# The conditioning product beside the RWKV-7 prompt scan: column-tiled fp32 matmuls against a high/low split on GpSimd

## The reference, cut to what matters

```
mod = jax.nn.silu(c) @ lp['w_ada'] + lp['b_ada']          # (9, 1024) @ (1024, 6144)
fm = jax.nn.silu(c) @ w_ada_f + b_ada_f                   # (9, 1024) @ (1024, 2048)
```

```
def step(S, inp):
    r_t, d_t, k_t, v_t, kk_t, b_t = inp
    sk = jnp.einsum('bhvk,bhk->bhv', S, kk_t)
    S = S * d_t[:, :, None, :] - sk[..., None] * b_t[:, :, None, :] + v_t[..., None] * k_t[:, :, None, :]
    return S, jnp.einsum('bhvk,bhk->bhv', S, r_t)
```

## Time and profile before

| what | value |
|---|---|
| time, median of 3 | 4452.27 us |
| the profiled execution | 4452.27 us, span 4450.7 us |
| mean granted TensorE clock, whole span | 0.969 of full speed |
| phase of the change | 752 to 1085 us, 333 us |
| PE busy in the phase | 303.76 us |
| DVE, ACT, POOL busy in the phase | 153.09, 64.83, 1.38 us |
| product records on PE (L1354) | 256 |
| granted clock in the phase | 0.97 |

### The profile page before, as it was taken

The page is one execution under the profiler, slowest core; times in us unless marked ns, Lnnn a source line. Parts: engine busy times, 40 slices in busy tenths (PEclk is TensorE's granted clock), DMA queues, the critical chain, the costliest instruction groups (busy, mean ns, idle before and its releaser), DMA issues. The chain is left out here.

```text
span 4450.7 us, 85485 instructions
## 1 busy us (share of the span) xinstructions
PE 4178.9 (94%) x32575; PEld 3796.1 (85%) x32575; DVE 3177.0 (71%) x6008; ACT 1431.2 (32%) x2183; POOL 1364.5 (31%) x1063
## 2 busy tenths in 40 slices
PE   7999999988778989999999998899999999999997
PEld 4889888887547879878888887899999999999996
DVE  5631344444844248899976665899999999999997
ACT  2221222211644222233346674222222222222223
POOL 6433331000032200054433233333434434434430
PEclk9999999999869999999999999999999999999998
DMA  4655666555533311144435546899999999999994
GB/s 169 208 191 188 205 227 207 192 219 165 154 118 115 123 63 34 51 142 142 143 119 189 193 176 254 294 301 300 301 301 301 302 299 299 303 299 300 303 299 151
DMA packets 523004, 928.00 MB, mean 209 GB/s; under 512 B 284032, under 2 KB 351232, under 8 KB 518688
## 3 DMA queue, kind: packets, MB, share of 16 engines
q1 hardware_dynamic: 387024, 549.29, 37.5%
q0 software_dynamic: 80960, 346.96, 22.8%
q10 hardware_dynamic: 54816, 28.85, 2.2%
HBM read 785.79 MB, written 206.30 MB: 223 GB/s over the span
## 5 line engine op out<-in xcount | busy, mean ns | idle before, releaser
L3296 POOL DMA_INDIRECT ex_rows<-expert_rows,ex_here x512 | 585.5, 1144 | 962.9 <-DVE acc_tok L3431 871.8
L3431 DVE SCALAR_TENSOR_TENSOR acc_tok<-ex_rows,ex_wsp,acc_tok 128x1024 f32<-128x1024 f32 x512 | 634.0, 1279 | 0.2 <-issue 0.2
L2663 PE MATMUL ex_psa<-x_dense_high,eg_u_high 128*128 128x288 f32 x2048 | 605.4, 296 | 9.3 <-ACT ex_w L3359 6.2
L2663 PE MATMUL ex_psa<-x_dense_low,eg_u_high 128*128 128x288 f32 x2048 | 605.4, 296 | 0.0
L2663 PE MATMUL ex_psa<-x_dense_high,eg_u_low 128*128 128x288 f32 x2048 | 605.0, 295 | 0.0
L2754 POOL TENSOR_TENSOR eg_u_low<-eg_u,eg_u_high 128x1024 fp32r<-128x1024 f32 x130 | 330.3, 2541 | 800.0 <-ACT eg_u_high L2749 800.0
L3328 PE MATMUL ex_pso<-ex_w_high,ex_v_high 128*128 128x288 f32 x2048 | 440.9, 297 | 20.0 <-DVE acc L3413 19.6
L3359 ACT ACTIVATE ex_w<-ex_psa 128x288 f32<-128x288 f32 x256 | 105.2, 411 | 1056.0 <-PE ex_psa L2663 1046.8
L3328 PE MATMUL ex_pso<-ex_w_high,ex_v_low 128*128 128x288 f32 x2048 | 439.4, 296 | 0.0
L3328 PE MATMUL ex_pso<-ex_w_low,ex_v_high 128*128 128x288 f32 x2048 | 438.3, 296 | 0.0
L3413 DVE TENSOR_TENSOR acc<-ex_pso,acc 128x576 f32<-128x576 f32 x512 | 373.9, 751 | 47.7 <-PE ex_pso L3328 47.7
(11 more groups left out here) (510 smaller groups left out, 9214.7 us busy)
## 6 DMA issues: line engine op xcount, KB each, us to landing
eg_u<-in_u SPq DMA_DIRECT2D x256, 512.0 KB, 3.3
expert_rows<-in_v SPq DMA_DIRECT2D x128, 512.0 KB, 7.0
ex_v<-in_v SPq DMA_DIRECT2D x128, 512.0 KB
weights<-wt_stage SPq DMA_DIRECT2D x9, 4096.0 KB, 13.0
ex_g<-weights SPq DMA_DIRECT2D x128, 288.0 KB
expert_rows<-eg_act SPq DMA_DIRECT2D x256, 128.0 KB, 1.7
proj<-in_out POOLq DMA_DIRECT2D x50, 548.5 KB, 6.2
in_w<-in_w_in SPq DMA_DIRECT2D x50, 512.0 KB, 4.7
```

The costliest lines, as they stand in the source:

```text
L2663: yield nc.tensor.matmul(out[:, 0:b - a], w[:, kc, :], half[:, kc, a:b], start=n == 0, stop=n == len(passes) - 1)
L3296: pool.indirect_dma_start(rows[i][:, :], None, table, index(here[par][:, t, j:j + 1]), element_offset=ROW_RUNS[t][0]).then_inc(s_row[i], 16)
L3431: v.scalar_tensor_tensor(out=acc_tok[:, t, :], in0=rows[i][:, at:at + D], scalar=wsp[:, i:i + 1], in1=acc_tok[:, t, :], op0=ALU.mult, op1= ...
```

## The change

The product is now computed from fp32r operands, without column groups. `cond` becomes 18 columns wide: 9 with the high part of the silu'd vectors and 9 with the low part. The weights are split too: POOL makes `wah` (rounded copy, fp32r) and then `wal` (weights minus `wah`), which lies on the same bytes as `wa`. That is eight copies and eight subtractions of 128x384 for each of 16 chunks. PE multiplies the 18 columns by both, 16 matmuls of 384 columns a chunk into 18 partitions; `fold` is now 18x9 and adds the two halves. PE waits for the subtractions (`s_al`) where it waited for the load (`s_wa`), and each half of the product is now 8 matmuls of fp32r instead of 4 of fp32. `k.clear_retired()` moves behind the split of chunk 1 in POOL's queue.

```diff
-        wa = [sb(f"ada{i}", [P, KC, ADA_STEP * P]) for i in range(2)]
-        cond = sb("cond", [P, KC, COL_TILE])
-        fold = sb("fold", [P, COL_TILE])
+        wa, wal = zip(*[(sb(f"ada{i}", [P, KC, ADA_STEP * P]), k.twin(f"rwc_ada_low{i}", [P, KC, ADA_STEP * P])) for i in range(2)])
+        wah = [ctx.enter_context(nc.sbuf_tensor(f"rwc_ada_high{i}", [P, KC, ADA_STEP * P], F32R)) for i in range(2)]
+        cond = ctx.enter_context(nc.sbuf_tensor("rwc_cond", [P, KC, 2 * NCOND], F32R))
+        fold = sb("fold", [2 * NCOND, NCOND])
...
-        row = sb("ada_row", [P, ACOLS])
-        rowp = b.ps[:, BANK_MOD, 0:ACOLS]
+        row = sb("ada_row", [2 * NCOND, ACOLS])
+        rowp = b.ps[0:2 * NCOND, BANK_MOD, 0:ACOLS]
...
-                g.memset(cond[:, :, :], 0.0).then_inc(s_cond, 1)
-                pool.wait_ge(s_cond, 1)
                 g.tensor_copy(cond[:, :, 0:NCOND], k.cT[:, :, :]).then_inc(s_cond, 1)
-                for q in range(COL_TILES):
...
-                pool.wait_ge(s_cond, 2 + COL_TILES)
-                k.clear_retired()
+                g.tensor_tensor(fold[:, :], k.ident[0:2 * NCOND, 0:NCOND], k.ident[0:2 * NCOND, NCOND:2 * NCOND], ALU.add).then_inc(s_cond, 1)
+                pool.wait_ge(s_cond, 2)
+                g.tensor_tensor(cond[:, :, NCOND:2 * NCOND], k.cT[:, :, :], cond[:, :, 0:NCOND].bitcast(F32), ALU.subtract).then_inc(s_cond, 1)
+                for c in range(NCH):
+                    pool.wait_ge(s_wa[c % 2], 16 * (c // 2) + 16)
+                    for kc in range(KC):
+                        g.tensor_copy(wah[c % 2][:, kc, :], wa[c % 2][:, kc, :]).then_inc(s_ah, 1)
+                    for kc in range(KC):
+                        pool.wait_ge(s_ah, KC * c + kc + 1)
+                        g.tensor_tensor(wal[c % 2][:, kc, :], wa[c % 2][:, kc, :], wah[c % 2][:, kc, :].bitcast(F32),
+                                        ALU.subtract).then_inc(s_al, 1)
+                    if c == 1:
+                        k.clear_retired()
...
-                        rest = (nc.tensor.matmul(rowp[COL_TILE * q:COL_TILE * q + COL_TILE, :], cond[:, j + q, :], wa[h][:, j + q, :],
-                                                 start=j == 0, stop=j == KC - COL_TILES)
-                                for j in range(0, KC, COL_TILES) for q in range(COL_TILES))
+                        rest = (nc.tensor.matmul(rowp, cond[:, kc, :], part[:, kc, :], start=kc == 0 and part is wah[h],
+                                                 stop=kc == KC - 1 and part is wal[h])
+                                for kc in range(KC) for part in (wah[h], wal[h]))
...
-                        pe.wait_ge(s_wa[h], 16 * r + 16)
-                        pe.wait_ge(s_cond, 2 + COL_TILES)
+                        pe.wait_ge(s_al, KC * (2 * r + h + 1))
+                        pe.wait_ge(s_cond, 3)
...
-                        for _ in range(COL_TILES):
+                        for _ in range(KC):
                             next(rest)
...
-                            mm = nc.tensor.matmul(modp[:, m, :], row[:, m * P:(m + 1) * P], fold[:, 0:NCOND],
+                            mm = nc.tensor.matmul(modp[:, m, :], row[:, m * P:(m + 1) * P], fold[:, :],
                                                   start=True, stop=True)
```

More of the change, by code:

```diff
@@ L152, in lasting @@
         return self.ctx.enter_context(self.nc.sbuf_tensor(name, shape, dt))
-COL_TILE = 32
-COL_TILES = P // COL_TILE
 ADA_FIRST = 16
@@ L1262, in phase_rw_prompt @@
         s_init = k.sem("rwc_state_zeroed")
-        s_cond = k.sem("rwc_cond_padded")
+        s_cond = k.sem("rwc_cond_split")
+        s_ah = k.sem("rwc_ada_high_made")
+        s_al = k.sem("rwc_ada_low_made")
         heads = [(p_, rows) for p_ in range(NPAIR) for rows in halves()]
@@ L1337, in _ @@
                 g = nc.gpsimd
-                g.memset(cond[:, :, :], 0.0).then_inc(s_cond, 1)
-                pool.wait_ge(s_cond, 1)
                 g.tensor_copy(cond[:, :, 0:NCOND], k.cT[:, :, :]).then_inc(s_cond, 1)
-                for q in range(COL_TILES):
-                    part = slice(COL_TILE * q, COL_TILE * q + COL_TILE)
-                    pool.wait_ge(s_cond, 2 + q)
-                    g.tensor_copy(fold[part, :], k.ident[part, part]).then_inc(s_cond, 1)
-                pool.wait_ge(s_cond, 2 + COL_TILES)
-                k.clear_retired()
+                g.tensor_tensor(fold[:, :], k.ident[0:2 * NCOND, 0:NCOND], k.ident[0:2 * NCOND, NCOND:2 * NCOND], ALU.add).then_inc(s_cond, 1)
[11 more added lines that the diff above has]
+                        k.clear_retired()
             @block.tensor
```

## The result

The changed kernel takes 4471.68 us (median of 9 runs, 4467.71 to 4487.97) against 4452.27 us for the kernel before (9 runs on the same chip, 4439.77 to 4462.12). The ratio is 1.0055, with a 95% interval of 1.004 to 1.0069: 18 to 31 us more, 24.5 us by the ratio and 19.4 us by the two medians. The two differ because the ratio rests on more executions: the record has 38 of the changed kernel, 4460.05 to 4493.20 us with a median of 4476.9. It is slower, and less so than the forecast of 4486 us; it lies inside the range. The profiled execution after took 4473.9 us, its mean granted clock was 0.967.

A forecast was written before the change was run, and what follows sets the result against it. The prediction took PE to bound the phase and added 22.4 us for the longer product and 12 us for POOL beside DVE to 4452.3 us, giving 4487; it named 4486 us, own range 4474 to 4501, 8-in-10 range 4466 to 4504.

The forecast's parts named there:

- PE is the full queue: In the changed phase PE, busy 303.76 of 333 us, sets the pace; longer matmul groups are paid almost whole.
- The product, +22.4 us: Conditioning product on PE: each half takes 1.49 us, 0.70 more, over 32 halves; bounds +18.5 to +24.3 us.
- Fold, row copy and bias at nothing: Steps after the product: fold matmuls and ACT's copy out of PSUM cost nothing more; bias only moves with the product.
- POOL's split and the wait on it: POOL's copies and subtractions take 13.3 us a chunk; PE's wait for them never binds, 5 us of cover left.
- POOL beside DVE, +12 us: POOL's instructions block DVE lines with two SBUF inputs, delaying PE 1.7 us in each of seven rounds; bounds 3.5 to 24.
- The 0.5 for the `tmp` line of h = 1 itself: In each round, the DVE line the product waits for loses 0.5 us to a POOL instruction.
- The 0.2 a round for lines behind the product: Delay of DVE's `xy` and `ml` lines after the product, counted at 0.2 us a round.
- No other phase changed: Expected sign in the changed profile: this phase 30 to 38 us longer, all other phases as before.
- Hidden: Rival: PE's idle time and PE work absorb most of the extra time; 4452 to 4470 us, chance 0.18.
- DVE the bound: Rival: blocking hits every two-input DVE instruction on the chain, or PSUM readers too; about 4515 us, chance 0.10.
- The split late: Rival: POOL, held up by DVE, needs over 17.6 us a chunk and PE waits; about 4509 us, chance 0.05.
- Faster: Rival: longer matmuls remove PE's idle time from instruction supply, with the product's extra inside it; about 4430 us, chance 0.03.

The follow-up runs named there:

- e7: The changed kernel with every half product computed twice, the second pass overwriting the first with the same values; 4526.97 us, ratio 1.0179.
- e2: The changed kernel, but POOL rounds only the weights of chunks 0 and 1, twice each, and PE uses those for all chunks; 4465.78 us, ratio 1.003.
- e5: The changed kernel with POOL's subtractions of odd chunks from 3 on held until the `tmp` line before the next product is done; 4471.98 us, ratio 1.005.
- e1: The kernel before with POOL's copies and subtractions added, their result unused and the product as it was; 4463.92 us, ratio 1.0021.
- e8: The kernel before with 24 POOL memsets of 128x384 a chunk added, which write SBUF and read none; 4448.59 us, ratio 0.9995.
- e6: The changed kernel with POOL's split in pieces four times as wide, two copies and two subtractions a chunk; 4488.31 us, ratio 1.0088.
- e3: The changed kernel with a hold on POOL's odd-chunk subtractions that named a round too early and held nothing; 4477.63 us, ratio 1.0055.

## Why the prediction was right, and where its sizes were off

**PE is the full queue: right.** e7 is the direct proof: 44.8 us of matmul time more made the rounds 48.4 us longer, 45.3 without what the clock and the `tmp` line changed. One of the readings behind it was not what it seemed: the 6.6 us in the earlier trace rows are waits of the weight load, which overlaps PE's work; PE's own waits for `ml` were 1.0 us in the same phase.

**The product, +22.4 us: right in its size on PE.** The pitch is 0.17 us and half a product 1.475 to 1.504 us in 28 of 31 groups. Two halves took 2.47 and 1.79 us, the first of them at a granted clock of 0.5, and the last group is a whole chunk's product. The sum of all halves went from 26.5 (mean of two executions) to 48.9 us, +22.4. (The upper bound of its sum should read 24.0, not 24.3.) What stays open is the time by the ratio of e2, 6 to 20 us with 13 in the middle, where the trace has 22. The profiled execution of e2 was at the slow end of its runs (4480.8 us; its runs reach from 4453.72 to 4482.06), so the two may differ by scatter alone. No term of the trace shows a gain of that size.

**Fold, row copy and bias at nothing: right.** L1417 takes 252 ns in the median, 257 before, and ACT's busy time in the phase is 65 us, as before.

**POOL's split and the wait on it: right.** 507 and 999 ns against 0.50 and 1.00 predicted; 12 to 13 us a chunk, mostly 12.1, without the 0.08 us between instructions that were estimated; loads land in 7.4 us. The tightest chunk is the last, as predicted: its subtractions ended at 1073.69 and the product started at 1081.23, 7.5 us of cover where 5 were worked out.

```profile
1070.57 3.12 POOL L1349 TENSOR_TENSOR rwc_ada_low<-rwc_ada,rwc_ada_high 128x384 fp32r<-128x384 f32 x2
```

```profile
1081.23 0.35 PE L1360 MATMUL rwc_ps<-rwc_ada_high,rwc_cond 128*18 128x384 f32 x1
```

**POOL beside DVE, +12 us: the right mechanism, mis-sized.** This is the step of the sum that was off. The `tmp` line is where it hurts, as predicted, and e5 shows that it is: held away from that line, the wait is 0. But it cost 5.2 us, 0.74 in each of the seven rounds that the sum counts, where it had 1 + 0.5 = 1.5. One of the seven had no wait, and the full price was met only where the subtractions lay right over the three lines of h = 0 (1.65 us at 863.36, 1.8 us at most). The 0.5 for the `tmp` line of h = 1 itself was too much: in the six rounds with a wait it was stretched by 0.35 us at most, and in the round shown POOL had just ended. The 0.2 a round for lines behind the product is confirmed as small, 0.2 us in all in the changed kernel and 0.8 in e5. What the sum did not have is the stretch ahead of the first product, where POOL splits chunks 0 and 1 and nothing but the chain of levels runs: 2.4 us of idle time more. Together 5.2 + 0.2 + 2.4 = 7.8 us for 12, within the bounds of 3.5 and 24, and the nearness of the two owes something to luck, since 2.4 us of it were in no term; e1 measures POOL's part alone at 9 us (3 to 16).

The Trainium skill, "SBUF — State Buffer", section "Who interferes with whom", says that a DVE instruction with two SBUF inputs contends with a GpSimd instruction that reads SBUF and not with one that only writes it. By that rule, the traces agree on both halves: L1128 reaches 949 ns beside reads (e1) and 418 ns beside writes (e8), and L1147, which reads PSUM, has 690 ns at most in the changed kernel.

**The sum.** With the measured sizes 22.4 + 7.8 = 30 us, less 1.9 us of idle time and with some clock; the two kernels differ by 18 to 31 us. The forecast of 34 us is above that. The phase was 24.9 and 29.3 us longer than in the two executions before, where 30 to 38 were named. "No other phase changed" can't be read from two profiles, since the rest of the program scatters by about as much. One more sign came only in part: PE's waits for the `tmp` line are 5.2 us, less than the 6.6 named, and the weight load's row for `ml` fell from 6.6 to 4.1.

**The rivals.** *Hidden*: against it stands e7. Idle time without a releaser was 20.4 us in the changed kernel, 22.5 in e2 and 23.0 in e7, with 20.7 and 23.9 in the unchanged one; no run shows that longer matmuls used it up. *DVE the bound*: no, but e6 goes its way. DVE lost 29 us of its own time and PE waited for 8 of them; with POOL instructions of 3.5 us it is 63 us, and the kernel ends at 1.0088. *The split late*: never, by at least 7.5 us. *Faster*: no sign of it. What the idle time without a releaser is made of stays open.

No kernel here beats the one before. A high/low product that keeps the four column groups, which might be the way to a cheaper product, was not tried.

## What to carry to other kernels

Price a matmul on the full engine by its start-to-start pitch times its count, and expect to pay all of it; idle time that stands next to it is not a reserve until a run shows that it shrinks. Before giving an idle engine work, ask what it shares with a busy one: the split's copies and subtractions cost time through reads of SBUF, 160 us of writes stretched no DVE line, and short instructions cost less than long ones with the same work (the whole change costs 24 us with short ones and 39 with long ones, by the ratios). And look for the one place where the delayed engine has no room, since nearly all of the stretched time elsewhere (29 us in all, 8 of them paid) was free.

## What was not expected of the hardware

A DVE instruction can lose to POOL more than once: 4.00 us for a line of 0.41 us, past four subtractions of about 1 us (e3). The estimate that it loses one instruction at most was wrong as an upper bound, though it held for nearly all others.

After PE had stood for some microseconds its granted clock fell to 0.5, 1.2 GHz, and the matmul groups behind took 0.48 us for 0.34 (e6, at 770). Such stretches also come in the unchanged kernel, 3.4 us or more of clock in its rounds, behind idle time of 1 to 3 us. One of the three in the rounds of the changed kernel begins right behind the longest wait for the `tmp` line (1.83 us, to 902.6) and makes the half product there 2.47 us long. So a wait of PE can cost more than its own length. But the loss does not go by the waits: the rounds lost 8.5 us to the clock in e2, which has no more waits than the kernel before, 8.5 in e3 and e5, 10.2 in e6 and 11.9 in e7, against 5.1 in the changed kernel and in e8 and 3.4 and 5.1 before. Why some profiles have more such stretches than others is not shown.

A wait told as "for POOL" at the product was none: its releaser had been done for 18 us. The end of the named instruction has to be looked up before such a row is believed.
